# Turned forms of a block inverse: from a second matmul and a copy to VectorE's block transposition

## The chip, the cores and the metric

The kernel runs on one core of a Trainium2 chip. The metric is the device time of one execution in microseconds (us). A core has the engines PE (TensorE: matmuls, with its weight loads PEld), DVE (VectorE), ACT (ScalarE), POOL (GpSimd) and SP (SyncE, which here issues the DMAs). Each runs its own instructions in the order in which they are written; between engines they are ordered by semaphores. SBUF is the working memory, PSUM the memory that matmuls write.

## The reference

One decoder layer with two groups of heads, for 16 meta tokens and 512 tokens of width 2048. After an RMS norm, one projection makes the columns of both groups. Eight pairs of heads of 64 do the RWKV-7 time mixing, in which each token updates a state of 64x64 for each head:

```python
def step(S, inp):
    r_t, w_t, k_t, v_t, kk_t, b_t = inp
    sa = jnp.einsum('bhvk,bhk->bhv', S, -kk_t)
    S = S * w_t[:, :, None, :] + sa[..., None] * b_t[:, :, None, :] + v_t[..., None] * k_t[:, :, None, :]
    y = jnp.einsum('bhvk,bhk->bhv', S, r_t)
    return S, y
```

The result gets a group norm, a bonus term and a gate. The other group, eight heads of differential attention, has a softmax of its own. Both go through an output projection, a norm and the residual. All inputs and the output are float32.

## The kernel before, in words

**Stages.** `ITER` lists 18 iterations. Each of the first 16 projects four tiles of 128 columns, for one pair of heads, while the pair projected in the iteration before is worked on. Iterations 1 to 8 have the work "rwkv" (the iterations that matter here), 9 to 16 "attn". The output projection follows, its first part in the last iteration.

**The projection** is PE's steady work. `feature_tile` (line 527) multiplies a tile of weights, split into a high and a low part (ACT's line 863 and POOL's line 1135, one unit of four feature tiles at a time), with the split activations, in three parts. A full tile has two matmuls of 264 columns in each part, another has one of 512. After a unit ACT may convert the next weights; after four units a projected tile is taken over by ACT (line 913) and DVE (line 1279).

**The rwkv work** cuts the 576 positions (528 tokens behind 48 of padding) into 9 chunks of 64, in 3 groups of 3 (`GC`, `NG`). A chunk of two heads is a block-diagonal matrix of 128x128 with two blocks of 64. For each group, `inv_pe`, `inv_dve` and `inv_act` make the inverse of a triangular matrix for its three chunks side by side (128x384): 24 groups in all. `chain_pe`, `chain_dve` and `chain_act` then take the state through the chunks one after another: matmuls at lines 709 (g), 714 (u) and 719 (s), with DVE's copies at lines 1451, 1456 and 1466 or 1468 between them. The chain of one group runs beside the inversion of the next, and that of the last group beside group 0 of the following iteration.

**The inversion** doubles the size of the inverted diagonal blocks at each level. `x16` holds the running inverse X, `xt16` its turned form. DVE masks the products (lines 1399, twice), takes the f16 form (1409) and makes level 0 into `xt16` (1411). PE turns it by a matmul with the identity (line 633), and ACT copies the result into `x16` (994). Then for each level l of 1 to 5: PE multiplies the level's masked matrix with X (643); DVE adds the identity into `z16` (1427) and masks the next level's matrix (1411); PE makes X from `xt16` and `z16` (660), and the turned X from `z16` and `xt16` (667); ACT copies both (1019 and 1022). A last correction follows (673 to 682). At levels 2 and 3 DVE also masks the k corners (1422). At level 1 PE turns b and k into the second bank of `ma`, in group 0 at levels 2 to 4 v, and ACT copies these out (1003, 1014 and 1015).

**The order.** On each engine the work of the parts is interleaved by hand: each part is a generator that yields a place, and `upto` issues whatever is due by the place reached. A place is one feature tile on PE (a third of one at best), and four for each unit. `inv_at(g, step)` gives places of 1.13 for each step, a level has two steps. On DVE the group norm of the pair before (`gn_dve`, lines 1304 to 1315), the stage (`stage_dve`, which prepares the factors of a pair), the bonus product (1376), the chain and the takeover of projected tiles lie between the steps of the inversion. In group 0 the bonus product and the takeover of xk stand between level 1's masking and line 1427; in group 1 the group norm's variance (1304) stands right behind level 0, POOL's power (1150), ACT's spread (943) and PE's turning (577) follow from it; in group 2 the takeover of xr stands between level 0 and level 1. The chain's places are `chain_at(g, 3c + k)`, which is `inv_at` of the next group at step 4.75 + 3c + k.

Of the kernel before, what the change touches and what calls it, by code (L numbers as in the profile page):

```python
# [31 lines left out]
ACT = mybir.ActivationFunctionType  # L32
# [17 lines left out]
GC = 3  # L50
# [63 lines left out]
LEVELS = 6  # L114
# [9 lines left out]
def hybrid_layer(nc, x, meta_tokens, pre_norm_w, w_in, rwkv_mu, rwkv_w0, rwkv_w_up, rwkv_a0, rwkv_a_up,  # L124
# [3 lines left out]
    with ctx:  # L128
# [87 lines left out]
        x16 = carve("rwkv", "x16", GC * P, F16)  # L216
        xt16 = carve("rwkv", "xt16", GC * P, F16)
        z16 = carve("rwkv", "z16", GC * P, F16)
# [49 lines left out]
        ident, ident16 = c32v("ident"), c16v(0)  # L268
# [11 lines left out]
        def s(name):  # L280
            if name not in S:
                S[name] = sem(name)
            return S[name]
# [23 lines left out]
        def inv_at(g, step):  # L307
            return INV_AT + INV_SPAN * g + INV_SPAN * step / INV_STEPS
# [205 lines left out]
        def _(pe):  # L514
            mm = nc.tensor.matmul
# [96 lines left out]
            def inv_pe(i, g):  # L612
                n = groups_so_far(i, g)
                cs = [g * GC + c for c in range(GC)]
                bl = lambda v, c: v[:, c * P:(c + 1) * P]
                bank = lambda k, c: ma[:, k * 512 + c * P:k * 512 + (c + 1) * P]
                yield inv_at(g, 0)
                if g == 0:
                    pe.wait_ge(s("pads_made"), (i - 1) * NG + 1)
                    pe.wait_ge(s("z_tanh"), i)  # L620
                else:
                    pe.wait_ge(s("pads_made"), (i - 1) * NG + g + 1)
                    pe.wait_ge(s("inv_taken"), n - 1)
                for c in range(GC):
                    for h, rows in enumerate(halves):
                        last = mm(ma[:, h * 512 + c * P:h * 512 + (c + 1) * P].rearrange("p (k t) -> p k t", k=2),  # L626
                                  bk[rows, cs[c], :], ar5[rows, cs[c], :, h, :], start=True, stop=True)
                last.then_inc(s("ab_done"), 1)
                yield inv_at(g, 2.2)
                pe.wait_ge(s("kb_copied"), n)  # L630
                pe.wait_ge(s("first_made"), n)
                for c in range(GC):
                    last = mm(bank(0, c), bl(xt16, c), ident16, start=True, stop=True)
                last.then_inc(s("t0_done"), 1)
                for l in range(1, LEVELS):
                    yield inv_at(g, 1.2 + 2 * l)
                    if l == 1:
                        pe.wait_ge(s("t0_taken"), n)
                    else:
                        pe.wait_ge(s("x_taken"), n * 5 + (l - 1 - 5))  # L640
                    pe.wait_ge(s("level_made"), n * 5 + (l - 5))
                    for c in range(GC):
                        last = mm(bank(0, c), bl(lv, (l - 1) * GC + c), bl(x16, c), start=True, stop=True)  # L643
                    last.then_inc(s("zz_done"), 1)
                    if l > 1:
                        pe.wait_ge(s("xt_taken"), n * 5 + (l - 1 - 5))
                    vg = v_turn(g, l)
                    if l == 1:
                        for c in range(GC):
                            if cs[c] < SC:  # L650
                                last = nc.tensor.transpose(bank(1, c), bk[:, cs[c], :], ident)
                        last.then_inc(s("bk_turned"), 1)
                    elif vg is not None:
                        for c, ch in enumerate(V_PAIRS[vg]):
                            last = nc.tensor.transpose(bank(1, c), xv[:, ch * CH:(ch + 2) * CH], ident)
                        last.then_inc(s("v_turned"), 1)
                    yield inv_at(g, 2.2 + 2 * l)
                    pe.wait_ge(s("zz_taken"), n * 5 + (l - 5))
                    for c in range(GC):
                        last = mm(bank(0, c), bl(xt16, c), bl(z16, c), start=True, stop=True)  # L660
                    last.then_inc(s("x_done"), 1)
                    if l == 1:
                        pe.wait_ge(s("bk_taken"), n)
                    elif vg is not None:
                        pe.wait_ge(s("v_taken"), (i - 1) * NV + vg + 1)
                    for c in range(GC):
                        last = mm(bank(1, c), bl(z16, c), bl(xt16, c), start=True, stop=True)  # L667
                    last.then_inc(s("xt_done"), 1)
                yield inv_at(g, 13.2)
                pe.wait_ge(s("x_taken"), n * 5)  # L670
                pe.wait_ge(s("lo_kept"), n)
                for c in range(GC):
                    mm(bank(0, c), bl(ab_hi, c), bl(x16, c), start=True, stop=False)
                    mm(bank(0, c), bl(ab_lo, c), bl(x16, c), start=False, stop=False)
                    last = mm(bank(0, c), minus16, bl(x16, c), start=False, stop=True)
                last.then_inc(s("r_done"), 1)
                yield inv_at(g, 14.2)
                pe.wait_ge(s("xt_taken"), n * 5)
                pe.wait_ge(s("r_taken"), n)
                for c in range(GC):  # L680
                    mm(bank(1, c), bl(x16, c), ident16, start=True, stop=False)
                    last = mm(bank(1, c), bl(r16, c), bl(xt16, c), start=False, stop=True)
                last.then_inc(s("inv_done"), 1)
# [171 lines left out]
        def _(act):  # L855
# [125 lines left out]
            def inv_act(i, g):  # L981
                b = g % 2
                n = groups_so_far(i, g)
                W = GC * P
# [4 lines left out]
                    src = ma[other, h * 512:h * 512 + W].rearrange("p (c k t) -> p c k t", c=GC, k=2)  # L989
                    last = A(ar5[other, g * GC:(g + 1) * GC, :, h, :], src, ACT.Copy)  # L990
                last.then_inc(s("kb_copied"), 1)
                yield inv_at(g, 2.7)
                act.wait_ge(s("t0_done"), n)
                A(x16, ma[:, 0:W], ACT.Copy).then_inc(s("t0_taken"), 1)
                for l in range(1, LEVELS):
                    vg = v_turn(g, l)
                    if l == 1:
# [19 lines left out]
                    yield inv_at(g, 2.7 + 2 * l)  # L1017
                    act.wait_ge(s("x_done"), n * 5 + (l - 5))
                    A(x16, ma[:, 0:W], ACT.Copy).then_inc(s("x_taken"), 1)  # L1019
                    yield inv_at(g, 2.9 + 2 * l)  # L1020
                    act.wait_ge(s("xt_done"), n * 5 + (l - 5))
                    A(xt16, ma[:, 512:512 + W], ACT.Copy).then_inc(s("xt_taken"), 1)  # L1022

            def chain_act(i, g, late, work, gn):
                n = groups_so_far(i, g, late)
# [160 lines left out]
        def _(dve):  # L1186
# [201 lines left out]
            def inv_dve(i, g):  # L1388
# [20 lines left out]
                steps(TT(g3(ab_hi), ab32, every(ident16), ALU.subtract))  # L1409
                l4 = lv.rearrange("p (l c t) -> p l c t", l=LEVELS - 1, c=GC)  # L1410
                level = lambda l, o: TT(o, g3(ab_hi), every(level_masks[:, l, :]), ALU.mult)  # L1411
                level(0, g3(xt16)).then_inc(s("first_made"), 1)
                yield inv_at(g, LEVEL_1)
                level(1, l4[:, 0]).then_inc(s("level_made"), 1)
                cs = slice(g * GC, (g + 1) * GC)
# [8 lines left out]
                for l in range(1, LEVELS):  # L1424
# [8 lines left out]
                    if l in MASK_AFTER:  # L1433
                        yield inv_at(g, 2.6 + 2 * l)
                        dve.wait_ge(s("kb_copied"), n)
                        mask_k(MASK_AFTER.index(l))
                yield inv_at(g, 13.7)
                dve.wait_ge(s("r_done"), n)
                TT(g3(r16), g3(ma[:, 0:W]), every(ident16), ALU.add).then_inc(s("r_taken"), 1)
# [182 lines left out]
```

## Time and profile before

| | us |
|---|---|
| median of 3 runs | 1470.88 |
| lowest, highest | 1467.04, 1473.22 |
| the profiled execution | 1466.28 |
| its span, first to last instruction | 1464.5 |

| engine | busy us | share of the span | instructions |
|---|---|---|---|
| PE | 1341.8 | 92% | 9393 |
| DVE | 725.9 | 50% | 1595 |
| ACT | 663.3 | 45% | 1518 |
| POOL | 476.0 | 32% | 362 |

The trace comes from the profiled execution. Durations are those of single instructions; matmuls overlap, so their distance from start to start says what one costs. In a row of the timeline, the square brackets hold the idle time of the engine just before the instruction and what ended it; "L660" is line 660 of the kernel.

### The profile page before, as it was taken

What the parts mean: (1) busy time and instruction counts of PE and PEld (TensorE: products, weight loads), DVE (VectorE), ACT (ScalarE), POOL (GpSimd) and SP (SyncE); (2) the same over time, 40 slices, a digit from 0 to 9 for tenths busy, and PEclk for the clock granted to TensorE, in tenths of its full rate; (3) what the DMA queues carried; (4) which work ended last, traced back from release to release, by engine and by line L of the source; (5) the groups of instructions that cost most, each with busy time, mean ns of one, the idle gap of its engine ahead of it and who ended that gap; (6) DMA issues with size and microseconds to landing.
All of it is one profiled execution on the core that took longest, in us unless ns stands there. A gap on an engine that the chain in (4) does not pass through costs nothing.

```text
span 1464.5 us, 23920 instructions
## 1 busy us (share of the span) xinstructions
PE 1341.8 (92%) x9393; PEld 1143.6 (78%) x9393; DVE 725.9 (50%) x1595; ACT 663.3 (45%) x1518; POOL 476.0 (32%) x362
## 2 busy tenths in 40 slices
PE   4999989989899898998989998999999999989997
PEld 3987778777787777877768786888888888668885
DVE  5335566656656666656666543444434444540013
ACT  4334545455455454554545463444444534432221
POOL 2342222322223222222222232343333343334443
PEclk9999999999999999999999999999999999999999
DMA  5221111211111111111111121222222222225433
GB/s 201 79 85 44 51 46 44 59 38 44 48 45 52 43 46 51 45 48 49 44 51 45 51 74 51 80 73 73 74 79 72 73 72 73 73 63 174 148 98 137
DMA packets 151263, 102.23 MB, mean 70 GB/s; under 512 B 6398, under 2 KB 140640, under 8 KB 149600
## 3 DMA queue, kind: packets, MB, share of 16 engines
q1 hardware_dynamic: 151152, 100.71, 23.1%
q8 instruction: 75, 1.23, 0.3%
q14 instruction: 36, 0.29, 0.1%
HBM read 96.49 MB, written 4.19 MB: 69 GB/s over the span
## 4 chain that ended last, share of the span: by engine, by line
PE 74%; DVE 17%; ACT 4%; issue 2%; POOL 2%; DMA 0%; DVEq 0%; ACTq 0%; SPq 0%
PE tile L527 41%; PE tile L793 2%; DVE arena L1411 2%; PE tile L795 2%; PE tile L794 2%; PE ma L643 2%; DVE arena L1399 2%; PE ma L759 2%; DVE arena L1345 2%; PE mb L709 1%; PE ma L667 1%; PE ma L660 1%; PE mb L774 1%; POOL arena L1150 1%; DVE arena L1355 1%
## 5 line engine op out<-in xcount | busy, mean ns | idle before, releaser
L1135 POOL TENSOR_TENSOR w_lo<-w_raw,w_hi 128x512 fp32r<-128x512 f32 x324 | 426.8, 1318 | 920.5 <-ACT w_hi L863 920.5
L527 PE MATMUL tile<-hn_hi,w_hi 128*128 128x264 f32 (+1 forms) x1696 | 452.3, 330 | 0.3
L527 PE MATMUL tile<-hn_lo,w_hi 128*128 128x264 f32 (+1 forms) x1696 | 438.0, 321 | 0.3
L527 PE MATMUL tile<-hn_hi,w_lo 128*128 128x264 f32 (+1 forms) x1696 | 437.3, 321 | 0.0
L863 ACT CAST w_hi<-w_raw 128x512 fp32r<-128x512 f32 x324 | 200.6, 619 | 350.8 <-PE tile L527 242.8
L527 PEld LDWEIGHTS tile<-hn_hi,w_hi 128*128 128x128 f32 x1696 | 278.7, 191 | 33.4 <-issue 13.9
L527 PEld LDWEIGHTS tile<-hn_lo,w_hi 128*128 128x128 f32 x1696 | 277.2, 190 | 15.4 <-issue 3.8
L527 PEld LDWEIGHTS tile<-hn_hi,w_lo 128*128 128x128 f32 x1696 | 277.3, 191 | 13.4 <-issue 0.4
L1427 DVE TENSOR_TENSOR arena<-ma,c 128x384 f16<-128x384 f32 x120 | 66.8, 557 | 46.5 <-PE ma L643 45.5
L1019 ACT ACTIVATE arena<-ma 128x384 f16<-128x384 f32 x120 | 58.9, 491 | 49.3 <-PE ma L660 47.0
L1411 DVE TENSOR_TENSOR arena<-arena,c 128x384 f16<-128x384 f16 x144 | 65.8, 462 | 0.8
L1150 POOL TENSOR_TENSOR arena<-arena,power 128x10 f32<-128x10 f32 (+3 forms) x28 | 43.9, 1569 | 47.9 <-DVE arena L1304 27.7
L1022 ACT ACTIVATE arena<-ma 128x384 f16<-128x384 f32 x120 | 58.1, 484 | 0.0
L793 PE MATMUL tile<-w_hi,hn_hi 128*128 128x512 f32 x128 | 52.5, 410 | 5.5 <-DVE hn_lo L1546 5.5
L990 ACT ACTIVATE arena<-ma 64x384 f32<-64x384 f32 x48 | 23.6, 491 | 60.3 <-PE ma L626 60.1
L795 PE MATMUL tile<-w_hi,hn_lo 128*128 128x512 f32 x128 | 50.8, 397 | 0.0
L794 PE MATMUL tile<-w_lo,hn_hi 128*128 128x512 f32 x128 | 50.8, 397 | 0.0
L660 PE MATMUL ma<-arena 128*128 128x128 f16 x360 | 41.7, 224 | 8.0 <-DVE arena L1427 8.0
L1528 DVE COPY arena<-mb 128x128 f32<-128x128 f32 x32 | 9.3, 292 | 78.3 <-PE mb L776 78.3
L1515 DVE TENSOR_TENSOR ma<-ma,c 128x128 f32<-128x128 f32 x32 | 9.6, 299 | 75.9 <-PE mb L759 75.8
L1466 DVE SCALAR_TENSOR_TENSOR arena<-mb,arena 64x64 f32<-64x64 f32 x112 | 31.7, 283 | 31.2 <-PE mb L719 29.8
L643 PE MATMUL ma<-arena 128*128 128x128 f16 x360 | 41.5, 224 | 5.6 <-ACT arena L1019 3.2
(248 smaller groups left out, 2127.0 us busy)
## 6 DMA issues: line engine op xcount, KB each, us to landing
w_raw<-w_in SPq DMA_DIRECT2D x260, 256.0 KB, 2.8
w_raw<-w_out SPq DMA_DIRECT2D x64, 256.0 KB, 3.0
big<-x SPq DMA_DIRECT2D x4, 1024.0 KB, 7.9
arena<-x SPq DMA_DIRECT2D x4, 1024.0 KB, 8.7
out<-big SPq DMA_DIRECT2D x3, 1024.0 KB, 3.9
arena<-post_norm_w SPq DMA_DIRECT2D x1, 1024.0 KB, 5.0
out<-big SPq DMA_DIRECT2D x2, 512.0 KB, 3.2
arena<-table_rope SPq DMA_DIRECT2D x2, 264.0 KB, 2.8
```

Source lines behind the costliest of these rows:

```text
L527: last = mm(o[:, at:at + n], w[:, slot, cols], t[:, kt, tok:tok + n], start=(kt == 0 and w is w_hi and t is hn_hi), stop=(kt == KT - 1 and ...
L643: last = mm(bank(0, c), bl(lv, (l - 1) * GC + c), bl(x16, c), start=True, stop=True)
L793: mm(banks[t], hn_hi[:, k, y], w_hi[:, k % RING, :], start=(k == 0), stop=False)
L794: mm(banks[t], hn_hi[:, k, y], w_lo[:, k % RING, :], start=False, stop=False)
L795: last = mm(banks[t], hn_lo[:, k, y], w_hi[:, k % RING, :], start=False, stop=(k == KT - 1))
L863: nc.scalar.copy(w_hi[:, slot, :], w_raw[:, slot, :]).then_inc(s("hi_done"), 1)
L1019: A(x16, ma[:, 0:W], ACT.Copy).then_inc(s("x_taken"), 1)
L1022: A(xt16, ma[:, 512:512 + W], ACT.Copy).then_inc(s("xt_taken"), 1)
L1135: T(w_lo[:, slot, :], w_raw[:, slot, :], w_hi[:, slot, :].bitcast(F32), ALU.subtract).then_inc(s("lo_done"), 1)
L1150: T(out_[:, 0:w], in_[:, 0:w], power[:, 0:w], ALU.pow).then_inc(s(name), 1)
L1411: level = lambda l, o: TT(o, g3(ab_hi), every(level_masks[:, l, :]), ALU.mult)
L1427: TT(g3(z16), g3(ma[:, 0:W]), every(ident16), ALU.add).then_inc(s("zz_taken"), 1)
```

## The change

`x16` is now made from level 0 by DVE's block transposition, which turns each 32x32 block in its place. After levels 1 to 4 DVE makes `xt16` from `x16` in the same way, behind a wait for ACT's copy of X (`x_taken`). Up to level 4 the running inverse is zero outside its diagonal 32x32 blocks. Level 5's turned form, with blocks of 64, still comes from the matmul and ACT's copy. PE's matmul for level 0 and its copy, and the matmuls and copies of the turned form at levels 1 to 4, are gone. PE waits for the transposition before it makes the next X. Of the waits for the second bank, that for b and k stands at level 2 now, and v's of level 2 is gone.

```diff
@@ inv_pe
-                yield inv_at(g, 2.2)
-                pe.wait_ge(s("kb_copied"), n)
-                pe.wait_ge(s("first_made"), n)
-                for c in range(GC):
-                    last = mm(bank(0, c), bl(xt16, c), ident16, start=True, stop=True)
-                last.then_inc(s("t0_done"), 1)
                 for l in range(1, LEVELS):
                     yield inv_at(g, 1.2 + 2 * l)
                     if l == 1:
-                        pe.wait_ge(s("t0_taken"), n)
+                        pe.wait_ge(s("kb_copied"), n)
+                        pe.wait_ge(s("first_turned"), n)
                     else:
                         pe.wait_ge(s("x_taken"), n * 5 + (l - 1 - 5))
...
-                    if l > 1:
-                        pe.wait_ge(s("xt_taken"), n * 5 + (l - 1 - 5))
...
                     yield inv_at(g, 2.2 + 2 * l)
                     pe.wait_ge(s("zz_taken"), n * 5 + (l - 5))
+                    if l > 1:
+                        pe.wait_ge(s("x_turned_here"), n * 4 + (l - 1 - 4))
...
-                    if l == 1:
+                    if l == 2:
                         pe.wait_ge(s("bk_taken"), n)
                     elif vg is not None:
                         pe.wait_ge(s("v_taken"), (i - 1) * NV + vg + 1)
-                    for c in range(GC):
-                        last = mm(bank(1, c), bl(z16, c), bl(xt16, c), start=True, stop=True)
-                    last.then_inc(s("xt_done"), 1)
+                    if l == LEVELS - 1:
+                        for c in range(GC):
+                            last = mm(bank(1, c), bl(z16, c), bl(xt16, c), start=True, stop=True)
+                        last.then_inc(s("xt_done"), 1)
...
-                pe.wait_ge(s("xt_taken"), n * 5)
+                pe.wait_ge(s("xt_taken"), n)
@@ inv_act
-                yield inv_at(g, 2.7)
-                act.wait_ge(s("t0_done"), n)
-                A(x16, ma[:, 0:W], ACT.Copy).then_inc(s("t0_taken"), 1)
...
-                    yield inv_at(g, 2.9 + 2 * l)
-                    act.wait_ge(s("xt_done"), n * 5 + (l - 5))
-                    A(xt16, ma[:, 512:512 + W], ACT.Copy).then_inc(s("xt_taken"), 1)
+                yield inv_at(g, 13.1)
+                act.wait_ge(s("xt_done"), n)
+                A(xt16, ma[:, 512:512 + W], ACT.Copy).then_inc(s("xt_taken"), 1)
@@ inv_dve
-                level(0, g3(xt16)).then_inc(s("first_made"), 1)
+                steps(level(0, g3(xt16)))
+                V.transpose(x16, xt16).then_inc(s("first_turned"), 1)
...
+                    if l < LEVELS - 1:
+                        yield inv_at(g, 2.8 + 2 * l)
+                        dve.wait_ge(s("x_taken"), n * 5 + (l - 5))
+                        V.transpose(xt16, x16).then_inc(s("x_turned_here"), 1)
```

## Rows read from the trace of the kernel before

**Rows 1.** Page, part 1: busy us (share of the span) and instructions per engine.

```profile
PE 1341.8 (92%) x9393; PEld 1143.6 (78%) x9393; DVE 725.9 (50%) x1595; ACT 663.3 (45%) x1518; POOL 476.0 (32%) x362
```

**Rows 2.** Busy time by stretch, one rwkv iteration: stretch, length, engines, PEclk, DMA share, GB/s.

```profile
389.00:482.00 93.00, 83.19 (x699) 72.03 (x698) 58.22 (x131) 47.55 (x112) 24.68 (x18) 1.00 0.16 47
```

**Rows 3.** PE's waits, whole span: who waited for whom, us in total, times, longest.

```profile
PE ma L633 <- DVE arena L1411: 18.6, 16, 1.6
...
PE mb L577 <- ACT tanh_g L943: 8.4, 8, 1.1
```

**Rows 4.** Groups by line and form: xcount, busy us, mean ns, idle before and its releaser.

```profile
L1427 DVE TENSOR_TENSOR arena<-ma,c 128x384 f16<-128x384 f32 x120 | 66.8, 557 | 46.5 <-PE ma L643 45.5
L1411 DVE TENSOR_TENSOR arena<-arena,c 128x384 f16<-128x384 f16 x144 | 65.8, 462 | 0.8
...
L1409 DVE TENSOR_TENSOR arena<-arena,c 128x384 f16<-128x384 f32 x24 | 13.4, 559 | 0.8
...
L1022 ACT ACTIVATE arena<-ma 128x384 f16<-128x384 f32 x120 | 58.1, 484 | 0.0
...
L994 ACT ACTIVATE arena<-ma 128x384 f16<-128x384 f32 x24 | 11.7, 487 | 48.3 <-PE ma L633 48.2
```

**Rows 5.** Line 1411 on DVE: count, min/median/max ns, first and last start.

```profile
L1411 DVE TENSOR_TENSOR arena<-arena,c x144: 347/350/1416, 115.7 to 825.2; 128x384 f16<-128x384 f16 x144
```

**Rows 6.** Timeline (start, us, engine, line), PE at level 1 of group 0 of one iteration.

```profile
394.80 0.34 PE L667 MATMUL ma<-arena 128*128 128x128 f16 x3
...
394.95 0.49 PE L527 MATMUL tile<-hn_lo,w_hi 128*128 128x264 f32 x2
```

**Rows 7.** Timeline, start of group 0's inversion in the same iteration.

```profile
390.37 0.63 DVE L1411 TENSOR_TENSOR arena<-arena,c 128x384 f16<-128x384 f16 x2
...
390.88 0.33 PE L633 MATMUL ma<-c,arena 128*128 128x128 f16 x3 [1.37 <-DVE arena L1411]
...
392.07 0.35 PE L643 MATMUL ma<-arena 128*128 128x128 f16 x3
...
392.60 0.70 ACT L913 ACTIVATE xk<-tile,om_mu 128x528 f32<-128x528 f32 x1
...
393.33 0.77 DVE L1279 SCALAR_TENSOR_TENSOR xk<-tile,par,xk 128x527 f32<-128x527 f32 x1 [1.60 <-ACT xk L913]
...
394.62 0.35 PE L660 MATMUL ma<-arena 128*128 128x128 f16 x3 [1.15 <-DVE arena L1427]
```

**Rows 8.** Timeline, level 2 of group 0, same iteration.

```profile
399.40 0.58 DVE L1466 SCALAR_TENSOR_TENSOR arena<-mb,arena 64x64 f32<-64x64 f32 x2 [0.82 <-PE mb L719]
...
399.63 0.49 ACT L1019 ACTIVATE arena<-ma 128x384 f16<-128x384 f32 x1
...
400.56 0.56 DVE L1427 TENSOR_TENSOR arena<-ma,c 128x384 f16<-128x384 f32 x1 [0.58 <-PE ma L643]
```

**Rows 9.** Timeline, start of group 1's inversion, same iteration.

```profile
416.86 1.68 POOL L1150 TENSOR_TENSOR arena<-arena,power 128x8 f32<-128x8 f32 x1 [3.96 <-DVE arena L1304]
...
419.26 0.66 PE L577 MATMUL mb<-c,tanh_g 128*128 128x128 f32 x4 [1.07 <-ACT tanh_g L943]
...
421.77 0.35 PE L660 MATMUL ma<-arena 128*128 128x128 f16 x3
```

**Rows 10.** Timeline, level 2 of group 1, same iteration.

```profile
425.15 1.54 DVE L1422 TENSOR_TENSOR arena<-arena,c 64x384 f32<-64x384 f32 x1
...
427.36 0.49 PE L709 MATMUL mb<-arena 128*128 128x128 f32 x2 [0.50 <-DVE arena L1468]
```

**Rows 11.** Timeline, start of group 2's inversion, same iteration.

```profile
442.31 1.26 POOL L1135 TENSOR_TENSOR w_lo<-w_raw,w_hi 128x512 fp32r<-128x512 f32 x1 [4.67 <-ACT w_hi L863]
...
442.39 1.40 DVE L1411 TENSOR_TENSOR arena<-arena,c 128x384 f16<-128x384 f16 x1
...
443.93 0.33 PE L633 MATMUL ma<-c,arena 128*128 128x128 f16 x3 [1.25 <-DVE arena L1411]
...
445.00 0.33 PE L643 MATMUL ma<-arena 128*128 128x128 f16 x3
```

## The prediction

> **What bounds the kernel now.** The page's first part comes first: PE (TensorE's matmuls) is busy 92% of the span, and DVE (VectorE) 50% [rows 1]. The whole is an average, so the stretches come next. The change touches only the eight rwkv iterations, and these repeat: each takes about 93 us, of which PE is busy 83, DVE 58 and ACT (ScalarE) 48, at a granted clock of 1.00, the level of 2.4 GHz [rows 2]. So PE sets the pace, with some ten microseconds of stalls per iteration. The list of PE's waits says where: the greatest single wait is the one this change takes away, the first turning (line 633) that waits for DVE's level 0 (line 1411), 18.6 us in 16 of the 24 groups; and 8.4 us go to the group norm's turning (line 577), which waits for ACT [rows 3]. Whether DVE may be given more work is read from the timeline of one iteration, group by group, since DVE's instructions run in written order: what counts is who stands behind a new wait there.
>
> **What is removed.** A group of three chunks loses five triples of f16 matmuls on PE: the first turning (line 633) and line 667 at levels 1 to 4. A triple holds PE for the 0.18 us from line 660 to line 667 [rows 7] or the 0.15 from there to the next feature matmuls [rows 6], so 0.17. Five by 24 groups by 0.17 is 20.4 us of PE time. ACT loses five copies of 128x384 for each group, at 484 to 487 ns [rows 4], 58 us in all. ACT is idle half the time, so this counts only where PE or DVE waits for a copy: line 994's result before level 1, gone. The copy of line 1019 stays and is as late as before.
>
> **What is added.** DVE gets five transpositions of 128x384 f16 for each group, 120 in all. No transposition is in the trace. Its nearest rows are the same shape at 559 ns (line 1409) and 557 ns (line 1427) [rows 4], and line 1411 with f16 on all sides, 350 ns when undisturbed [rows 5]. I take 0.56, since only line 1411, with f16 in and out, is faster than that, and nothing in the trace says that a transposition goes at its rate; 0.35 is the short end. For the long end I take 0.9: POOL is busy 25 of 93 us [rows 2], and if every meeting with it held a transposition up for a whole 1.26 us [rows 11], the mean would be 0.56 + 0.27 x 1.26 = 0.90. 120 by 0.56 is 67 us of DVE time, 8.4 us for each iteration on top of 58 of 93: room on average, so only its places matter.
>
> A page of the Trainium skill speaks on both. "VectorE: DVE Perf Modes", section "The three transpose paths", gives 311 ns for a 128x128 bf16 block transposition; an estimate from it, with 256 more columns at the 0.96 GHz of that page, is 0.58 us, and no run here shows it yet.
>
> **A busy neighbour.** Line 1411 took 1.40 us instead of 0.35 where POOL's line 1135 had begun 0.08 us before it [rows 11], and line 1422 took 1.54 [rows 10]: both read two SBUF tensors. On average line 1411 pays 462 ns [rows 4] for its 350 [rows 5]. The transposition reads one tensor; if it were also held up by POOL, it would pay about the same 0.11 us more on average. "SBUF — State Buffer" of the Trainium skill, section "Who interferes with whom", says so as a rule: a VectorE operation with two SBUF inputs, or in a two-port mode, locks out GpSimd and is locked out by it; one with a single input outside those modes isn't. By that rule the long level operations agree with the trace, and a transposition at full length would be free of it, while a fast two-port one would average 0.46 rather than 0.35.
>
> **Group 0: a gain at the start, and small ones later.** Before, PE stands 1.37 us at line 633 until 390.88, goes on to line 643 at 392.07, and then stands 1.15 us again at line 660 until 394.62 [rows 7]. That second wait hangs on a chain: the end of a weight unit on PE, ACT's line 913 (392.60, 0.70), DVE's line 1279 (393.33, 0.77), then line 1427 (0.56). After, PE isn't stopped at 389.5 (390.88 less 1.37), and the unit ends about 1.5 us earlier. DVE sets the time instead: level 0 ends at about 390.7, the transposition at 391.3, level 1 (0.35) at 391.7, the bonus product (about 0.7) at 392.4, line 1279 at 393.1, line 1427 at 393.7. So line 660 starts at 393.7 in place of 394.62: -0.9. At the levels PE gains 4 times 0.17 = 0.7. The new wait on DVE stands ahead of the chain's state copy (line 1466) at level 2: before, that copy ran at 399.40, but ACT's line 1019 ends only at 400.12, so the transposition would end at 400.7 and the copy at 401.3, against line 1427 at 400.56 [rows 8]. ACT and PE are by then about 0.6 ahead, which just covers it. The cover costs up to 0.7 if it is gone. Group 0 in all: -1.6.
>
> **Group 1: a loss at the start, and no gain later.** There ACT's copy of line 994 was late for another reason: POOL's power (line 1150, 416.86, 1.68) feeds ACT's spread, on which PE waits 1.07 us at line 577 until 419.26 [rows 9]. DVE's line 1304 feeds line 1150, and it stands right behind the transposition now. So all this comes 0.56 later, and line 660 moves from 421.77 to about 422.3. At levels 1 and 2 the group norm's products and the chain's copies stand behind the transposition, and PE already waits 0.50 us at line 709 for the state copy [rows 10]: DVE is the bound there, and the 0.7 us that PE saves are lost in its waits. Some comes back, since the 1.54 us of line 1422 should meet POOL at another moment, with up to 1.0 us to win, and as much can be lost at a level operation. I take +0.3 for the group, out of -0.4 to +0.9.
>
> **Group 2: a loss at the start, made good.** Line 1411 ends at 443.79, held up by POOL; line 633 stands 1.25 us until 443.93 and line 643 starts at 445.00 [rows 11]. After, DVE does the transposition (to 444.35), the token shift of xr (about 0.7, which stands between level 0 and level 1 in DVE's order) and level 1 (0.35): line 643 starts at 445.45, +0.45. The wait at line 633 isn't saved but moved to line 643. The levels give back 0.7, with no group norm here: -0.25 for the group.
>
> **The sum.** An iteration gains 1.6 - 0.3 + 0.25 = 1.55 us, and six of the eight are like this one: 9.3. The first (no group norm, so nothing of group 1's loss: about 2.5) and the last (about 1.7, since its group 0 isn't held by line 913) give 4.2. Together 13.5 us, of 20.4 that PE loses in work. The profiled execution had 1466.28 us, its span 1464.5; the median of the runs is 1470.88. Against the execution the sum gives 1452.8, and against the median, which I forecast, 1457.4. Nothing outside the eight iterations is touched.
>
> **The rivals.** *PE's order alone counts* (15%): the 20.4 us all arrive, and with them the 0.9 us of group 0's start in eight iterations, 7: 1443.5. For it speaks that PE is 92% busy; against it, the places in group 1 where PE waits for DVE already. *DVE takes back every level* (25%): only the starts count, -0.9 + 0.56 + 0.45 = +0.1 for each iteration, so +1 and 1472. For it speaks the new wait for ACT's line 1019, behind which line 1427 and both chain copies are queued, in each of 96 levels; against it, that the timeline leaves DVE idle for 0.5 to 1 us ahead of most of them. *A long transposition, slower than before* (13%): by the walk above the path goes through the transposition at about nine places of an iteration (three starts, two levels each in groups 0, 1 and 2), 72 in all. The forecast's gain is gone when it takes 0.56 + 13.5/72 = 0.75 us; at the long end, 0.9, the sum is -13.5 + 72 x 0.34 = +11, so 1482. Against it speaks that every 128x384 row takes 0.56 or less when POOL is quiet. *The change doesn't do what it says* (2%): block transposition equals the whole one only while all that isn't zero lies in the diagonal 32x32 blocks, which holds up to level 4; and level 5 keeps its matmul. No time would move by that: 1471.
>
> **How the numbers follow.** The forecast, 1457.4, has 45%, with its own range of 1449 to 1466. About 0.5% (7 us) is what a measurement of this kernel can tell from no change. Faster: the first rival and nearly all of the forecast, 58%. Same: the second rival, the last, and the rest of the forecast, 28%. Slower: the long transposition with a bit of a worse meeting with POOL, 14%. The range reaches to the first rival with a transposition shorter than 0.56, and on the other side past the second, but not to the whole of the slower case: 1440 to 1476.
>
> **What would show it.** A transposition's row at 0.5 to 0.6 us. No wait at line 633, and in its place one at the first matmuls of level 1 in groups 0 and 2 of over 1 us. The wait for line 1427 at 0.7 rather than 1.15 in group 0. The wait at line 577 longer by 0.6, and waits of line 709 and 714 on DVE's copies in group 1. An iteration of 91.7 us instead of 93.3. The prediction is wrong if transpositions last 0.75 or more, or if DVE's wait for line 1019 makes the chain of group 0 as late as that of group 1.

## The result, and the profile after

The changed kernel takes 1479.84 us (median of 11 runs, 1474.06 to 1488.83), the one before 1468.73 in the same comparison (11 runs, 1467.04 to 1473.22). The ratio is 1.0073 with a 95% interval of 1.0057 to 1.0090: 0.7% slower, where 1457.4 and a gain had been forecast, in a range that ended at 1476. The profiled execution took 1475.96 us against 1466.28.

The page's first part, after, against [rows 1]:

```profile
PE 1337.5 (91%) x9033; PEld 1137.4 (77%) x9033; DVE 782.3 (53%) x1715; ACT 617.4 (42%) x1398; POOL 474.5 (32%) x362
```

PE has 360 matmuls fewer and yet is busy for only 4 us less. The spans with their mean granted clock say why; first the changed kernel, then the one before:

```profile
core 0: 1474.2 us, clock 0.975
```

```profile
core 0: 1464.5 us, clock 0.989
```

The clock has two levels, 2.4 and 1.2 GHz, so a mean of 0.975 is 5% of the span, 74 us, at the lower one, against 32 us before. The low clock comes in spells of about 3.4 us, at times two or three end to end. A stretch of one iteration (its last figures are PEclk, DMA share and GB/s), after and before:

```profile
575.00:668.00 93.00, 82.21 (x641) 0.94 0.15 44
```

```profile
575.00:668.00 93.00, 84.63 (x698) 0.98 0.16 47
```

The transposition is as long as was assumed, in all 120 cases, and DVE waits 64 us in all for ACT's copy of X ahead of those at the levels. Two groups of the page, after (idle time before them and its releaser last):

```profile
L1434 DVE STREAM_TRANSPOSE arena<-arena 128x384 f16<-128x384 f16 x96 | 55.5, 578 | 65.7 <-ACT arena L1012 64.4
...
L638 PE MATMUL ma<-arena 128*128 128x128 f16 x360 | 41.6, 224 | 32.5 <-DVE arena L1404 28.6
```

PE's waits, after, against [rows 3] (lines have moved: 638 is the first matmul of a level, 643 before; 705 and 710 are the chain's g and u, 709 and 714 before; 655 is 660; on DVE 1404 is 1411 before, 1421 is 1427, 1297 is 1304, 1449, 1464 and 1466 are 1451, 1466 and 1468; 1406 and 1434 are the new transpositions):

```profile
PE ma L638 <- DVE arena L1404: 28.6, 17, 2.3
...
PE mb L577 <- ACT tanh_g L939: 14.3, 8, 1.9
...
PE mb L705 <- DVE arena L1466: 6.3, 7, 1.2
```

The wait at the first turning (18.6 us) is gone, and one of 28.6 us has come at level 1. Then the schedule, apart from the clock: the starts of the groups' first products (line 626) in the iteration of the prediction, groups 0, 1, 2, and group 0 of the next. Before:

```profile
384.34 1.66 PE L626 MATMUL ma<-arena 64*128 64x128 f32 x12 [2.03 <-DVE arena L1355]
...
413.49 0.94 PE L626 MATMUL ma<-arena 64*128 64x128 f32 x12
...
439.66 0.94 PE L626 MATMUL ma<-arena 64*128 64x128 f32 x12
...
477.64 0.94 PE L626 MATMUL ma<-arena 64*128 64x128 f32 x12 [2.03 <-DVE arena L1355]
```

After:

```profile
384.07 0.94 PE L626 MATMUL ma<-arena 64*128 64x128 f32 x12 [2.03 <-DVE arena L1348]
...
411.18 0.94 PE L626 MATMUL ma<-arena 64*128 64x128 f32 x12
...
438.78 0.94 PE L626 MATMUL ma<-arena 64*128 64x128 f32 x12
...
476.67 0.94 PE L626 MATMUL ma<-arena 64*128 64x128 f32 x12 [2.03 <-DVE arena L1348]
```

Group 0 went from 29.15 to 27.11 us (-2.04), group 1 from 26.17 to 27.60 (+1.43), group 2 from 37.98 to 37.89 (-0.09): 92.60 instead of 93.30, -0.70. No spell of the low clock lengthens a group here, but group 0 has one at its first products in both kernels. Before, the products themselves take 1.66 us instead of 0.94. After, the stretch with the first products has a mean clock of 0.72:

```profile
384.00:387.00 3.00, 2.67 (x20) 0.72 0.32 93
```

In the kernel before, group 0 is just as long in the iterations without it. In the changed kernel every group 0 of 27.1 us has it, and no run shows that kernel's group 0 without any spell; e9 below, the same kernel with further work in its stalls, has two such groups in the middle iterations, of 27.85 us, a gain of 1.3 us instead of 2.0.

Groups that no spell lengthens repeat these figures to 0.1 us in the other iterations too, but for the first, group 2 of the seventh and the last. Where the time went is read from the first products of the last group, before and after:

```profile
810.09 0.94 PE L626 MATMUL ma<-arena 64*128 64x128 f32 x12
```

```profile
813.91 0.94 PE L626 MATMUL ma<-arena 64*128 64x128 f32 x12
```

The changed kernel gets there 3.8 us later. Seven of its groups (groups 0 and 1 of the third rwkv iteration, 1 and 2 of the fifth, all three of the sixth) are longer than their like, by 7.5 us together, and each has a spell. Without that the schedule gained 3.7 us: 1.0 up to the start of the second iteration, 0.65 to 0.70 in each from there to the sixth, nothing in the seventh, and it lost 0.6 in the last; 0.7 x 8 would have been 5.6. From the start of the last group to the end of the span the program is the same in both kernels but for that one group, whose like differs by 0.1 us, and it takes 654.4 us before and 660.3 after: 5.9 us more, with 31 us at the low clock instead of 12. So the 9.7 us between the two spans are -3.7 of schedule, +7.5 in rwkv groups with a spell, and +5.9 behind them. Against the medians, 11 us apart, the clock took about 15.

### The profile page after: what moved, and what is told of

It reads as the page before. It is cut to its first block, busy times and chain, and to the rows that moved or that the text cites. A ratio compares the mean times of both kernels' runs of the same rounds, so it can differ in the third digit from the quotient of the medians.

```text
span 1474.2 us, 23272 instructions
## 1 busy us (share of the span) xinstructions
PE 1337.5 (91%) x9033; PEld 1137.4 (77%) x9033; DVE 782.3 (53%) x1715; ACT 617.4 (42%) x1398; POOL 474.5 (32%) x362
## 4 chain that ended last, share of the span: by engine, by line
PE 71%; DVE 20%; ACT 4%; issue 2%; POOL 2%; DMA 0%; DVEq 0%; ACTq 0%; SPq 0%
PE tile L527 40%; DVE arena L1404 3%; PE tile L789 2%; PE tile L790 2%; PE tile L791 2%; DVE arena L1392 2%; PE ma L638 2%; PE ma L755 2%; DVE arena L1338 2%; PE ma L655 1%; PE mb L705 1%; ACT w_hi L859 1%; PE mb L770 1%; DVE arena L1348 1%; POOL arena L1143 1%
## 5 line engine op out<-in xcount | busy, mean ns | idle before, releaser
L1434 DVE STREAM_TRANSPOSE arena<-arena 128x384 f16<-128x384 f16 x96 | 55.5, 578 | 65.7 <-ACT arena L1012 64.4
L1012 ACT ACTIVATE arena<-ma 128x384 f16<-128x384 f32 x120 | 58.9, 491 | 54.6 <-PE ma L655 52.2
L1404 DVE TENSOR_TENSOR arena<-arena,c 128x384 f16<-128x384 f16 x144 | 73.9, 513 | 0.8
L638 PE MATMUL ma<-arena 128*128 128x128 f16 x360 | 41.6, 224 | 32.5 <-DVE arena L1404 28.6
L638 PEld LDWEIGHTS ma<-arena 128*128 128x128 f16 x360 | 21.7, 99 | 51.6 <-issue 36.9
```

## The experiments

All times stand against the kernel before at 1468 to 1470 us. "On the schedule" means: read from the starts of line 626 (or its counterpart) in groups that no spell of the low clock lengthens, against the same groups before. In group 0 these are mostly groups with a spell at their first products. The place of a spell is given by its distance from the first products of its group, and "behind the last group" is the stretch from there to the end of the span. Clocks are those of the profiled executions.

**One part alone.** e1 keeps the matmul and copy for the turned form at levels 1 to 4 and does only the first turning on DVE; e2 does the opposite; e3 has the whole change in group 0 and nothing in groups 1 and 2.

```diff
+START_TURNED = (0, 1, 2)   # e1; () in e2; (0,) in e3
+LEVELS_TURNED = ()         # e1; (0, 1, 2) in e2; (0,) in e3
...
+if g not in START_TURNED:
+    yield inv_at(g, 2.2)
...
+    last.then_inc(s("t0_done"), 1)
```

> Only the first turning is done by DVE (with no matmul and no copy); levels 1 to 4 are as before the change. Theory A (the places in DVE's order decide: group 0 gains, groups 1 and 2 lose): from the changed kernel's trace, group 0 about -1.1 us up to the first X, group 1 +0.6, group 2 +0.6, so about 0 for each iteration and 1469 in all, if the granted clock stays at 0.989. Theory B (the matmuls that PE loses count): 24 x 0.17 = -4 us. Theory C (PE's clock is granted lower, because the stall of PE ahead of level 1 got longer): the clock falls towards the changed kernel's 0.975 and the time is some 8 us longer than before, though the schedule is even.

Measured: 1495.98 us, ratio 1.0175 (1.0156 to 1.0194), clock 0.966. A fifth of the removed matmuls and of the transpositions cost 26 us, more than twice what the whole change costs. On the schedule it looks even, as theory A had it: -1.1 and +0.6, and +0.6 for group 2, read from e7 below, since in e1 all eight groups 2 have a spell and lose 1.8 or more. But the -1.1 comes in groups 0 with a spell at their first products; without any, in e7, group 0 gains only 0.4, and the start alone then loses 0.8 us for each iteration. The clock fell, as theory C had it, though the forecast of 8 us was much too small.

> The first turning stays with PE and ACT; DVE turns X at levels 1 to 4. Theory A: group 0 -0.9, group 1 +0.8 (the chain's copies and the group norm behind the transposition), group 2 -0.7: -0.8 for each iteration, -6 us, 1463 at an unchanged clock. Theory B: 96 x 0.17 = -16 us. Theory C: the stall ahead of level 1 is as before, so the clock stays at about 0.989; if it falls all the same, the clock follows from something else.

Measured: 1460.56 us, ratio 0.9934 (0.9916 to 0.9953), clock 0.988. Theory A's 1463 is nearly met: -0.9, +0.8 and -0.7 on the schedule. So the half of the change that leaves the start of each group alone is a gain, and the clock stays.

> The change in group 0 alone; groups 1 and 2 are as before. Theory A: -2.0 us for each of eight iterations, -15 us, 1454. Theory that DVE's work costs wherever it is put: 40 of 120 transpositions, so a third of the changed kernel's loss, +3 us. Theory C: the clock as before, 0.985 or above.

Measured: 1464.09 us, ratio 0.9966 (0.9951 to 0.9981), clock 0.979. Group 1 is as before to 0.03 us, and so is group 2 but for the second, sixth and seventh iteration (+0.3, -1.0, +0.65). Group 0 gains its 2.0 in the second, fourth and sixth iteration, with a spell at its first products. In the third, fifth and seventh PE stands 2.16 us ahead of level 1, a spell begins 8.7 to 9.8 us into the group, and the gain is 0.3 or a loss of 0.7. Some 6 of the 10 us short of the forecast go there, and behind the last group the profiled run is 4 us longer than before the change. The expected clock of 0.985 was wrong.

**Is it the wait, or the length?** e4 puts the levels' transposition behind the chain's copy; e5 takes its wait away (it reads something always ready and writes a spare buffer; the turned form isn't updated); e6 keeps the wait and turns 32 columns instead of 384.

```diff
-                        yield inv_at(g, 2.8 + 2 * l)
+                        yield inv_at(g, 3.1 + 2 * l)                                  # e4
...
-                        dve.wait_ge(s("x_taken"), n * 5 + (l - 5))
-                        V.transpose(xt16, x16).then_inc(s("x_turned_here"), 1)
+                        V.transpose(spare16[:], ab_hi).then_inc(s("x_turned_here"), 1)  # e5
...
+                        V.transpose(xt16[:, 0:32], x16[:, 0:32]).then_inc(s("x_turned_here"), 1)  # e6
```

> The changed kernel with the transposition of levels 1 to 4 put behind the chain's copy on DVE (3.1 steps instead of 2.8). If the queueing of the chain's copies behind the wait for X's copy is what costs group 1 its 0.9 us after the first X, that goes: -0.9 for each iteration or -7 us against the changed kernel's 1480. If the length of the transposition alone costs, nothing changes (within 2 us).

Measured: 1487.21 us, ratio 1.0123 (1.0093 to 1.0153), clock 0.968 in the profile. Neither forecast held. In the sixth iteration, the only one whose groups aren't lengthened by a spell, the schedule is better than the changed kernel's (-2.4, +1.0, -0.4: -1.8 for an iteration instead of -0.7), by about the size that the queueing theory asked, but only 0.46 of the 1.1 us is in group 1, where that theory put it. Yet the time is 7 us longer: 20 of the 24 groups have a spell behind one of their long stalls. A better schedule, a worse clock.

> The changed kernel, but at levels 1 to 4 the transposition reads the f16 form of the products (always ready) and writes a spare buffer, so DVE doesn't wait for ACT's copy of X; the turned form isn't updated (that part of the computation is left out). The number and length of DVE's operations stay. If the wait with the chain's copies behind it costs group 1 its 0.9 us after the first X, that goes: -0.9 for each iteration, 1473. If the length costs, 1480. In either case the stall ahead of level 1 stays, and with it a clock near 0.975.

Measured: 1485.69 us, ratio 1.0111 (1.0070 to 1.0151), clock 0.964 in the profile. Group 1 is 1.70 us longer than before, with a spell in it that begins 7.7 us in; e9 below, which has the wait, has one group 1 with a spell at the same place, and it is also 1.70 longer. So the wait for X's copy costs group 1 nothing that the length doesn't cost anyway.

> The changed kernel with only the first 32 of 384 columns transposed at levels 1 to 4 (most of the turned form isn't updated), the wait kept; an operation should take about 0.2 us in place of 0.58. If the length costs, some 0.35 us at each of two or three places of group 1 come back, -0.9 for each iteration, 1473; if the wait alone costs, nothing, 1480. Clock near 0.975 in either case.

Measured: 1473.46 us, ratio 1.0036 (1.0019 to 1.0052), clock 0.969. The transposition at the levels, in e6:

```profile
L1434 DVE STREAM_TRANSPOSE arena<-arena 128x32 f16<-128x32 f16 x96 | 20.3, 212 | 68.2 <-ACT arena L1012 66.6
```

It is 0.37 us shorter, the wait as long as before (66.6 against 64.4 us). Group 1 without a spell lost 0.69 instead of 1.43, so twice the 0.37; group 0 gained 2.39 instead of 2.04 and group 2 0.36 instead of 0.09, once each. The length counts, at four levels of an iteration. The forecast of 1473 was met, in part by luck: the schedule gives 1.4 us for each iteration, not 0.9, and the low clock, 0.969, took some of it back.

**Is it the clock?** If the clock falls because PE stands ahead of level 1, work on PE that feeds nothing, put into that stall, should bring it back. e7 does this to e1, e9 to the changed kernel.

```diff
+                if g in (0, 2):
+                    yield inv_at(g, 3.1)
+                    pe.wait_ge(s("kb_copied"), n)
+                    pe.wait_ge(s("ab_taken"), n)
+                    for _ in range(6):
+                        for c in range(GC):
+                            mm(bank(0, c), ident16, ident16, start=True, stop=True)
```

> The kernel with the first turning alone on DVE (e1: 1496 us, clock 0.966), and 18 further f16 matmuls of 128 columns on PE, whose results aren't used, between the masking and level 1 in groups 0 and 2, where PE stands for about 2 us. They take 1.0 us of that stall and feed nothing. Theory C (the clock falls because PE stands there): the clock goes back to 0.98 or more and the time falls by 10 to 25 us, to 1471 to 1486, although PE has more to do. Rival (the clock has nothing to do with that stall, or costs nothing): 1496 to 1499.

Measured: 1484.04 us, ratio 1.0108 (1.0091 to 1.0125), clock 0.984. PE has 288 matmuls more than in e1 and the kernel is 12 us faster; in the profiled runs 7 of these lie in the rwkv iterations and 4 behind the last group. It is still 15 us slower than the kernel before: its schedule loses 0.8 us for each iteration, group 1, where nothing was put in, has a spell behind its stall of 1.91 us at the group norm's turning (line 577 before) in four iterations, and behind the last group it is 3 us longer. Group 2 of the fourth rwkv iteration in e1, in stretches of 3 us (length, PE busy, PEclk):

```profile
448.00:451.00 3.00, 3.00 (x29) 1.00 0.30 84
451.00:454.00 3.00, 1.54 (x7) 1.00 0.01 4
454.00:457.00 3.00, 2.21 (x14) 0.72 0.31 89
457.00:460.00 3.00, 3.00 (x17) 0.72 0.00 0
460.00:463.00 3.00, 3.00 (x24) 1.00 0.31 87
```

PE stands for 2.25 us, and the two stretches that hold the end of that stall and what follows it have a mean clock of 0.72: 0.28 x 2 of 6 us, or 3.4 us, at half the clock. The same group in e7, with the 18 matmuls in the stall:

```profile
445.00:448.00 3.00, 3.00 (x25) 1.00 0.11 32
448.00:451.00 3.00, 1.77 (x22) 1.00 0.24 67
451.00:454.00 3.00, 3.00 (x22) 1.00 0.09 26
454.00:457.00 3.00, 2.96 (x22) 1.00 0.21 63
```

No fall, and none in any of the eight groups 2 of e7, where e1 has one in each. And its price, from the first products of this group and of the next one, in e1 and then in e7:

```profile
448.81 0.94 PE L634 MATMUL ma<-arena 64*128 64x128 f32 x12
...
488.59 0.94 PE L634 MATMUL ma<-arena 64*128 64x128 f32 x12 [2.03 <-DVE arena L1379]
```

```profile
445.03 0.94 PE L635 MATMUL ma<-arena 64*128 64x128 f32 x12
...
483.61 0.94 PE L635 MATMUL ma<-arena 64*128 64x128 f32 x12 [2.03 <-DVE arena L1387]
```

39.78 us with a spell, 38.58 without: a spell costs this stage 1.2 us.

> The changed kernel with the 18 further matmuls of e7 ahead of level 1 in groups 0 and 2 (results not used). Theory C: the clock rises from 0.971 (median of its 11 runs) to 0.98 or more, and the time falls from 1480 to 1468 to 1474, since its schedule without spells of the low clock is about 5 us ahead of the kernel before. Rival (the slowdown is the schedule's): the clock may rise, but the time stays at 1480 or goes up by the further work.

Measured: 1473.46 us (1466.33 to 1477.28, 10 runs), ratio 1.0028 (1.0011 to 1.0044), clock 0.979 in the profile. As theory C asked: 288 matmuls that feed nothing make the changed kernel 6 us faster. In the profile no group 2 has a spell now (2 of 8 had one); groups 0 and 1 still have some, and group 1 was given no work.

> e8 (group 0 whole, group 2 at its levels, clock 0.979, 1463.7) with 24 further matmuls on PE, results not used, in group 0 just ahead of the first products, where PE stands for 2 us until DVE has made its factors. Theory C: the spell that e8's trace has in group 0 of nearly every iteration goes, the clock rises to 0.99 and the time falls by about 8 x 1.2 = 10 us to 1454. Rival: no change, or a little longer.

(Its matmuls stand ahead of line 626 in group 0, in the same form; e8, from which it starts, is below.) Measured: 1461.59 us, ratio 0.9946 (0.9930 to 0.9961), clock 0.984. The clock rose by 0.004 and the time fell by 2 us, but the spell in group 0 came in each iteration all the same, and this forecast missed. The trace says why: the work went into the wrong stall. It shortened the one ahead of the first products, from 2.03 to 0.68 us, but e8's spell begins 8.6 us or more into the group in all iterations but the fifth, behind a stall of 2.17 us ahead of level 1. That stall e11 left at 2.16 to 2.18 us. In e8, fourth iteration (first products at 382.07):

```profile
390.21 0.33 PE L655 MATMUL ma<-arena 128*128 128x128 f16 x3 [2.17 <-DVE arena L1435]
```

```profile
387.00:390.00 3.00, 1.04 (x9) 1.00 0.00 0
390.00:393.00 3.00, 2.79 (x18) 0.61 0.29 87
```

So e11 doesn't test the theory at the stall that matters. e7 and e9, whose work does go into that one, have no spell behind it in any group 0.

**The term of group 1's start.** e12 puts the group norm's variance (line 1304 before) ahead of the transposition.

```diff
                 steps(level(0, g3(xt16)))
+                if g == 1:
+                    yield inv_at(g, 0.9)
                 V.transpose(x16, xt16).then_inc(s("first_turned"), 1)
```

> The changed kernel with the group norm's variance ahead of group 1's first transposition in DVE's order. If group 1's loss up to the first X (+0.61 us) comes from POOL's power starting one transposition later, it goes to about 0: -0.6 for each of seven iterations, -4 us on the schedule; the rest of group 1's loss (+0.8 at levels 2 and 3) stays. The clock may move either way; the schedule is read group by group.

Measured: 1469.39 us (1460.01 to 1477.41, 10 runs), ratio 1.0004 (0.9979 to 1.0029), clock 0.981 in the profile. Up to the first X group 1 is where it was before the change (-0.04 instead of +0.61 us), and in all it loses 0.78 instead of 1.43. The schedule gains 5 us, the time 10, with a better clock. With the variance first, group 1's stall at line 577 is 1.26 us:

```profile
420.84 0.66 PE L577 MATMUL mb<-c,tanh_g 128*128 128x128 f32 x4 [1.26 <-ACT tanh_g L939]
```

No group 1 of this run has a spell. With the stall at 1.91 us one begins at 6.4 to 7.8 us in three groups 1 of the changed kernel and in five of e1. This is a second sign that a stall of about 2 us brings the spell, without any work that feeds nothing.

**Versions.** e8 has group 0 whole and group 2 at its levels; e10 has DVE turn X only at the levels, in groups 0 and 2.

```diff
+START_TURNED = (0,)     # e8; () in e10
+LEVELS_TURNED = (0, 2)  # both
```

> Turning by DVE where the traces show a gain only: group 0 in whole, group 2 at levels 1 to 4, group 1 not at all. Schedule: -2.0 and -0.7 for each iteration, -21 us; the clock as with group 0 alone (0.979, which there took some 10 us back), so 1457 in all; with the clock of the kernel before it would be 1448.

Measured: 1463.66 us, ratio 0.9962 (0.9947 to 0.9977), clock 0.980: 7 us short. Group 2 gives its 0.7 in each iteration but for the seventh; in the second to seventh iteration group 0 has a spell, mostly behind the stall of 2.17 us ahead of level 1, and gains 0.2 to 0.7 instead of 2.0.

> First turning by matmul and copy in all groups; DVE turns X at levels 1 to 4 of groups 0 and 2 only, group 1 as before the change. From e2's trace: -0.91 and -0.70 for each iteration and none of group 1's +0.82: -13 us at the clock of the kernel before, 1456; if each transposition costs wherever it is, no better than e2's 1460.6.

Measured: 1456.50 us (1455.94 to 1459.79), ratio 0.9916 (0.9892 to 0.9941), clock 0.986. This beats the kernel before by 0.8% and the changed one by 1.6%: -0.9 in group 0, nothing in group 1, -0.7 in group 2, in the second to sixth iteration (group 1 of the third loses 0.3). Behind the last group its profiled run takes 659.4 us, with 31 us at the low clock, as long as in the changed kernel: the loss there comes without any joined stall too.

## Why the prediction was wrong, point by point

**The removed matmuls, the added transpositions.** Right in size. Where 0.56 us was taken, the trace has (shortest, median and longest ns):

```profile
L1434 DVE STREAM_TRANSPOSE arena<-arena x96: 578/578/580, 121.7 to 831.1; 128x384 f16<-128x384 f16 x96
```

The estimate from the Trainium skill ("VectorE: DVE Perf Modes", "The three transpose paths"), 0.58, agrees with it. The Trainium skill's rule ("SBUF — State Buffer", "Who interferes with whom") agrees with the trace too: line 1404, with two inputs in SBUF, took 1.31 us beside POOL's 1.29, while all transpositions took the same time, though 37 of the 120 ran beside one of POOL's operations. The rival of a long transposition is therefore excluded. So are two others: *PE's order alone counts* by group 1, which lost 1.43 us, and *DVE takes back every level* by e2, where groups 0 and 2 keep 0.9 and 0.7 at their levels and only group 1 loses. Neither of the two signs by which the prediction called itself wrong came, a transposition of 0.75 us or a late chain in group 0.

**Group 0.** The mechanism was right, and the size is between two readings: -2.04 against -1.6 with a spell at the first products, -1.3 without any (e9). That the measured 2.0 is so near is in part luck. Timeline, after:

```profile
390.51 0.58 DVE L1406 STREAM_TRANSPOSE arena<-arena 128x384 f16<-128x384 f16 x1
...
391.47 0.33 PE L638 MATMUL ma<-arena 128*128 128x128 f16 x3 [0.67 <-DVE arena L1404]
...
393.24 0.35 PE L655 MATMUL ma<-arena 128*128 128x128 f16 x3 [0.37 <-DVE arena L1421]
...
398.19 0.58 DVE L1434 STREAM_TRANSPOSE arena<-arena 128x384 f16<-128x384 f16 x1 [1.16 <-ACT arena L1012]
...
398.69 0.54 DVE L1464 SCALAR_TENSOR_TENSOR arena<-mb,arena 64x64 f32<-64x64 f32 x2
```

From the end of level 0 to the first X the order is that of the prediction. The state copy behind the wait at level 2 (DVE stands 1.16 us there) comes 5.45 us behind the first X instead of 4.78, and PE shows no wait for it here. The sign of a wait of over 1 us at level 1 came in groups 2, and in group 0 only in two iterations of eight (2.16 us); here it is 0.67.

**Group 1.** The start was right: +0.61 where 0.56 was taken, and e12 shows that it is the variance behind the transposition. The levels were mis-sized: with +0.3 for the group, the working counted on the removed matmuls being just lost in waits and on a luckier meeting of line 1422 with POOL. Timeline, after:

```profile
414.31 0.58 DVE L1406 STREAM_TRANSPOSE arena<-arena 128x384 f16<-128x384 f16 x1
414.92 0.17 DVE L1297 TENSOR_SCALAR arena<-mb 128x8 f32<-128x8 f32 x1
...
417.56 0.66 PE L577 MATMUL mb<-c,tanh_g 128*128 128x128 f32 x4 [1.91 <-ACT tanh_g L939]
...
420.08 0.35 PE L655 MATMUL ma<-arena 128*128 128x128 f16 x3 [0.39 <-DVE arena L1421]
...
422.57 0.49 PE L710 MATMUL mb<-arena 128*128 128x128 f32 x2 [0.41 <-DVE arena L1449]
...
422.90 1.31 DVE L1404 TENSOR_TENSOR arena<-arena,c 128x384 f16<-128x384 f16 x1
...
426.66 0.49 PE L705 MATMUL mb<-arena 128*128 128x128 f32 x2 [0.80 <-DVE arena L1466]
```

The mask of the k corners did escape POOL (0.56 us), but level 3's masking met it instead, 1.31 us against 0.35, and with two transpositions in the line (e6: 0.37 us less of each gives 0.74 back) PE waits for the chain's copies at lines 710 and 705, 0.41 and 0.80 us. The group lost 1.43, outside the -0.4 to +0.9 that stood beside the +0.3. Named as the cause of such losses was the wait for ACT's copy too; e5 speaks against it (1.70 with a spell, whether DVE waits or not), though e4, with the transposition further back, has 0.46 less.

**Group 2.** The wait moved as said, to 2.25 us at level 1. Up to there the group lost 0.62 instead of 0.45, and the levels gave back 0.7; -0.09 against -0.25:

```profile
444.74 0.33 PE L638 MATMUL ma<-arena 128*128 128x128 f16 x3 [2.25 <-DVE arena L1404]
```

**The sum.** An iteration gains 0.70 us instead of 1.55, and the eight of the profiled run 3.7 us instead of 13.5. This is the mis-sized part: of the 0.85 us short in an iteration, group 1 has 1.13 and group 2 0.16, and group 0 gives 0.44 more than was said.

**The step that failed.** "The wait at line 633 isn't saved but moved to line 643" was priced at nothing beyond its length. Before, PE stood 1.25 us in group 2, had the turning and three parts of a feature tile to do, and went on; after, it stands 2.25 us in one piece. In the same way "all this comes 0.56 later" in group 1 was priced as a length, and made the stall at line 577 one of 1.91 us instead of 1.07. In e1 the clock falls right behind that stall of group 2 (0.5 us after its end in the fourth iteration), in e7, with work in the stall, it doesn't, and e7 and e9 are faster for such work by 12 and 6 us; in e12 a shorter stall at line 577 leaves group 1 without a spell. The prediction read the granted clock in one iteration (1.00 [rows 2]) and no rival asked what would become of it.

Its price comes out between 13 and 18 us. In the profiled pair it is 7.5 us in rwkv groups and 5.9 behind them, 13.4 in all. The 11 runs of the changed kernel go from 1474.06 us at 0.976 to 1488.83 at 0.962, 1.06 us for each 0.001; the medians of the clock are 0.971 and 0.988, so 18, an estimate. And the measured 11 us with the schedule's 3.7 make 15. Only the first part, the spells in rwkv groups, is tied to the stalls that the change lengthened. The runs above 1479 us (e1, e4, e5, e7 and the changed kernel) all have the first turning on DVE in all three groups. e6, e9 and e12 have it too and end at 1469 to 1473: with the short transposition, with work in the stalls, and with the shorter stall at line 577.

What stays open: which pattern of PE's work keeps the clock up. The stall of 2.25 us in group 2 is followed by a spell in 8 of 8 groups of e1 and of e5, but in 2 of 8 of the changed kernel and 3 of 8 of e12; that of 1.25 us, before the change and in e2, e3, e8 and e10, in none. Whether the length in one piece or the sum counts wasn't tested; for the piece speaks that the kernel before stands 1.54 and 1.15 us in group 0 of the second iteration, with the turning between them, and has no spell behind it, while e8 with one stall of 2.17 us has. The spells of the kernel before in group 0, in about half of its iterations, are others: they stand at the first products, and cost nothing. And why the attention and output stages have more of the low clock in some runs is open: e10, whose stalls are those of the kernel before, loses 5.0 us there; e12, whose groups 2 have the long one, 1.5.

## What to carry to other kernels

On a kernel in which PE is busy nine tenths of the time, look at how long its stalls are in one piece, not only at their sum: a stall that an edit lengthens from 1.1 or 1.25 us to 2 can cost more than the work that it removes, through the granted clock. Compare clocks of the runs before believing a schedule, and put the stages side by side where both are at the full clock, those whose program didn't change too: here more than a third of the clock's price lay there. When a stall is filled to test such a theory, look first at which stall the spell follows. And where an engine's order is written by hand, make such a change group by group: here the part worth having was the levels of two groups of three.

## What the runs showed of the hardware

A block transposition of f16 takes 212 ns for 32 columns and 578 for 384: 1.04 ns for each column and about 0.18 us besides, and POOL's work beside it doesn't lengthen it (578 to 580 ns in all 120 cases). A stall of PE of 2.25 us, in a kernel that is busy before and after it, was followed by a spell of 3.4 us at 1.2 GHz in each of 8 cases in e1, but in 2 of 8 in the changed kernel; with 18 small matmuls in it, in none of 8 in e7. A spell lengthened a group by 0.6 to 1.8 us, or, at the first products of group 0, by nothing. The same program's runs differ in mean clock (0.962 to 0.976), and their times with it.
